# A fused two-block kernel: the attention of block 1 rearranged (one merged tail unit, mask on TensorE, unnormalised differences, LayerNorm and half of the output product inside its steps)

## What is computed

```python
hn = rmsnorm(h, norm1_g[l])
q, k, v, u = split(hn @ w_in[l])                    # 4 heads; q, k: 2 components of 64; v: 128
q, k = apply_rope(q, cos, sin), apply_rope(k, cos, sin)
# differential attention, causal, by head:
s = einsum(q, k) * 0.125 ; s = where(k_pos <= q_pos, s, -inf)
p = softmax(s) ; a = p[:, :, 0] - lam * p[:, :, 1]
attn_out = rmsnorm(a @ v, sub_g) * (1 - lam_init)
# conformer branch: GLU, causal depthwise convolution of width 31, LayerNorm over 512 channels, swish
z = a_half * sigmoid(gate) ; z = conv31(z) + conv_b ; conv_out = silu(layer_norm(z, ln_g, ln_b))
h = h + concat([attn_out, conv_out]) @ w_out[l]     # 1024 x 1024
h = h + (silu(gate) * up) @ w_down[l]               # after a second rmsnorm
```

## Time and profile before

| | us |
|---|---|
| median of 3 runs | 3113.19 (3109.66 to 3121.58) |
| the profiled execution's own time | 3118.58 |
| its span | 3116.8 |
| busy in the span: PE / DVE / ACT / POOL | 2756.3 / 1144.6 / 980.7 / 1205.2 |
| mean granted clock of TensorE | 0.904 of full |

### The profile page before, as it was taken

The page is one execution under the profiler, slowest core; times in us unless marked ns, Lnnn a source line. Parts: engine busy times, 40 slices in busy tenths (PEclk is TensorE's granted clock), DMA queues, the critical chain, the costliest instruction groups (busy, mean ns, idle before and its releaser), DMA issues.

```text
span 3116.8 us, 47600 instructions
## 1 busy us (share of the span) xinstructions
PE 2756.3 (88%) x19056; PEld 2457.3 (79%) x19056; DVE 1144.6 (37%) x1879; ACT 980.7 (31%) x1841; POOL 1205.2 (39%) x511
## 2 busy tenths in 40 slices
PE   5977879999797787999978989889999989699999
PEld 4954879999796477999977868768877777577777
DVE  3874422112268443211224864320266632220110
ACT  2323222222332322222233542123456653221121
POOL 3550335545556023555552431022311135554452
PEclk8975889999898578999987989998999989899999
DMA  3210012232222001223230300031201123222221
GB/s 121 77 54 1 28 54 91 71 108 64 86 70 67 1 14 55 93 72 101 69 96 28 108 28 2 2 95 55 82 27 56 42 91 126 81 68 95 81 94 67
DMA packets 178614, 204.10 MB, mean 65 GB/s; under 512 B 6443, under 2 KB 167174, under 8 KB 178198
## 3 DMA queue, kind: packets, MB, share of 16 engines
q1 hardware_dynamic: 174288, 200.05, 19.9%
q10 hardware_dynamic: 4166, 1.84, 0.2%
HBM read 193.48 MB, written 8.39 MB: 65 GB/s over the span
## 4 chain that ended last, share of the span: by engine, by line
PE 68%; issue 10%; POOL 7%; DVE 7%; ACT 3%; POOLq 2%; DVEq 1%; DMA 1%; ACTq 1%; SPq 0%
PE ps L683 15%; PE ps L684 15%; PE ps L685 15%; PE ps L1431 6%; POOL wlo L2509 5%; PE ps L1321 2%; PE ps L832 2%; DVE top L2086 1%; PE ps L849 1%; PE ps L1303 1%; POOLq L2547 1%; DVE diff L2106 1%; PE ps L1266 1%; POOL hn_lo L2524 1%; PE ps L713 1%
## 5 line engine op out<-in xcount | busy, mean ns | idle before, releaser
L2509 POOL TENSOR_TENSOR wlo<-wraw,whi 128x2048 fp32r<-128x2048 f32 x182 | 836.9, 4599 | 1205.1 <-ACT whi L1498 1185.8
L683 PE MATMUL ps<-hn_hi,whi 128*128 128x264 f32 (+1 forms) x3008 | 972.8, 323 | 64.8 <-POOL hn_lo L2524 31.8
L684 PE MATMUL ps<-hn_lo,whi 128*128 128x264 f32 (+1 forms) x3008 | 958.8, 319 | 0.0
L685 PE MATMUL ps<-hn_hi,wlo 128*128 128x264 f32 (+1 forms) x3008 | 957.1, 318 | 0.0
L683 PEld LDWEIGHTS ps<-hn_hi,whi 128*128 128x128 f32 x3008 | 578.5, 192 | 105.5 <-issue 51.1
L685 PEld LDWEIGHTS ps<-hn_hi,wlo 128*128 128x128 f32 x3008 | 576.9, 192 | 36.4
L684 PEld LDWEIGHTS ps<-hn_lo,whi 128*128 128x128 f32 x3008 | 578.7, 192 | 32.0
L1498 ACT CAST whi<-wraw 128x2048 fp32r<-128x2048 f32 x182 | 346.7, 1905 | 730.5 <-PE ps L685 581.5
L683 PE MATMUL ps<-ff_hi,whi 128*128 128x264 f32 x704 | 200.7, 285 | 9.6 <-POOL ff_lo L2589 9.6
L685 PE MATMUL ps<-ff_hi,wlo 128*128 128x264 f32 x704 | 200.5, 285 | 0.0
L684 PE MATMUL ps<-ff_lo,whi 128*128 128x264 f32 x704 | 200.1, 284 | 0.0
(11 more groups left out here) (406 smaller groups left out, 4157.5 us busy)
## 6 DMA issues: line engine op xcount, KB each, us to landing
wraw<-in_w_in SPq DMA_DIRECT2D x54, 1024.0 KB, 5.3
wraw<-in_w_gate_up SPq DMA_DIRECT2D x44, 1024.0 KB, 5.1
wraw<-in_w_up SPq DMA_DIRECT2D x16, 1024.0 KB, 5.6
wraw<-in_w_down SPq DMA_DIRECT2D x16, 1024.0 KB, 4.9
wraw<-in_w_out SPq DMA_DIRECT2D x12, 1024.0 KB, 5.2
wraw<-in_w_down SPq DMA_DIRECT2D x16, 768.0 KB, 4.6
wraw<-in_w_down SPq DMA_DIRECT2D x16, 640.0 KB, 4.2
gate_dram<-gate_out SPq DMA_DIRECT2D x16, 256.0 KB, 2.1
```

What stands on the lines that cost most here:

```text
L683: nc.tensor.matmul(dst, whi[:, slot, c:c + P], rhs_hi, start=start, stop=False)
L684: nc.tensor.matmul(dst, whi[:, slot, c:c + P], rhs_lo, start=False, stop=False)
L685: return nc.tensor.matmul(dst, wlo[:, slot, c:c + P], rhs_hi, start=False, stop=stop)
L2509: nc.gpsimd.tensor_tensor(wlo[:, slot, :], wraw[:, slot, :], whi[:, slot, :].bitcast(F32), ALU.subtract).then_inc(w_split, 1)
```

## The change

- The four 16-query tiles of the heads become one unit: 17 units in place of 20. The unit stands twelfth (counted from 0) in the list. Its four heads lie in four groups of 32 partitions; the queries are kept in `q_tail`, written by DVE beside the rotary addition.
- The mask is added by PE, as a matmul with the identity behind the scores; DVE takes the maximum with its sign turned, and the scale 0.125 goes into ACT's copy of q, so two of DVE's operations per unit go.
- The first exponential is written in place in PSUM; the difference is (first exponential) + (second) x ratio, not normalised, one DVE operation after a reciprocal and a ratio. The head norm takes up the missing factor through the squared row sums (`mass_sq`).
- Rotations 0 to 2 stand between the last q and k products, rotation 3 behind them, rotations 4 to 7 inside units 1 to 4. The order of the q and k panels follows that.
- 12 taps of channel chunk 1 run on DVE ahead of pass 1's `z`.
- The LayerNorm's spread rows, squares and scaling run inside units 0 and 6 to 8. The output product is cut into 32 halves of 12 matmuls: the conv half of the inner dimension (16 of them) starts at unit 10, one piece in a unit, seven pieces in units 10 to 16; nine stand between the steps of the head norm, and the 16 of the attention half follow. DVE makes 32 additions to `h` instead of 16. The panels of the output weights are cut the other way (4 chunks of rows by 512 columns).
- The transposed differences and the outputs have one PSUM bank each, not two.
- ACT casts the last panel of the output product after the squares, not before.

```diff
@@ PE: what follows the q and k products, and the loop over units
+                            if f >= 23:
+                                rotated(f - 23)
...
+                def rotated(m):
+                    pe.wait_ge(qkv_copied, l * 26 + rot_from[m])
+                    if m:
+                        pe.wait_ge(rope_done, l * KD + m)
+                    if m == 4:
+                        pe.wait_ge(ln_mean_copied, l + 1)
+                    for half in range(2):
+                        last = nc.tensor.matmul(ps[:, rot_bank(m) + half, 0:HALF], rot,
+                                                raw(rot_chunks[m], HALF * half, HALF), start=True, stop=True)
...
+                    if u == TAIL:
+                        for c in range(2):
+                            for h1 in range(HEADS1):
+                                own = slice(32 * h1, 32 * h1 + 32)
+                                q = q_tail[:, c, h1, :]
+                                nc.tensor.matmul(ps[own, c, :], q, raw(4 + h1, 0, 512), start=True, stop=True)
...
                     for c in range(2):
                         own = slice(64 * c, 64 * c + 64)
+                        nc.tensor.matmul(ps[:, 2 * (u % 2) + c, 0:keys], raw(hd, P * t, P)[own, :], raw(4 + hd, 0, keys)[own, :],
+                                         start=True, stop=False, skip_group_check=True)
+                    for c in range(2):
+                        last = nc.tensor.matmul(ps[:, 2 * (u % 2) + c, P * t:keys], ident, causal, start=False, stop=True,
+                                                skip_group_check=True)
...
+                rotated(3)
+                conv_sums()
                 scores(0)
                 scores(1)
+                extras = {0: conv_mean_rows, 6: conv_square_sums, 7: conv_rstd_rows}
+                f = 0
+                for u in range(UNITS1):
+                    differences_turned(u)
+                    if u + 2 < UNITS1:
                         scores(u + 2)
+                    if u in extras:
+                        extras[u]()
+                    elif 1 <= u <= 4:
+                        rotated(u + 3)
+                    elif u >= 10:
+                        out_fill(f)
+                        f += 1
+                    values(u)
...
+                out_fill(7)
+                pe.wait_ge(sub_mass, l + 1)
+                nc.tensor.matmul(ps[:, 4, 0:4 * NT1], ident, mass_sq, start=True, stop=False, skip_group_check=True)
+                head_sums1(0)
+                head_sums1(1)
+                out_fill(8)
+                head_sums1(2)
+                out_fill(9)
+                head_sums1(3)
+                out_fill(10)
+                out_fill(11)
+                head_rows1(0)
+                head_rows1(1)
+                out_fill(12)
+                out_fill(13)
+                head_rows1(2)
+                out_fill(14)
+                head_rows1(3)
+                out_fill(15)
@@ ACT: exponentials
+                            p = probs4[:, u % 2, 1, 0:P * (t + 1)] if c else s[:, 0, :]
+                            last = nc.scalar.activation(p, s[:, c, :], ACT.Exp, bias=top, accum_out=mass[:, c, at:at + 1])
+                    act.drain().then_inc(exp_done, 1)
...
+                for u in range(UNITS1):
+                    if u + 1 < UNITS1:
+                        exponentials(u + 1)
+                    if u:
+                        out_copied(u - 1)
+                    differences_copied(u)
@@ DVE
+                        add_taps(1, range(MERGED))
...
+                    nc.vector.tensor_tensor(turned_half, turned_half, sin.rearrange("p (b n) -> p b n", b=2), ALU.mult)
...
+                    nc.vector.reciprocal(weight[:, slot:slot + 1], mass[:, 1, at:at + 1])
                     dve.drain()
+                    nc.vector.scalar_tensor_tensor(ratio[:, slot:slot + 1], mass[:, 0, at:at + 1], lay_neg_lam,
+                                                   weight[:, slot:slot + 1], ALU.mult, ALU.mult)
                     dve.drain()
+                    nc.vector.scalar_tensor_tensor(diff[:, slot, 0:keys], probs4[:, slot, 1, 0:keys], ratio[:, slot:slot + 1],
+                                                   scores_of(u)[:, 0, :], ALU.mult, ALU.add).then_inc(diff_ready, 1)
...
+                for m in range(4):
+                    rope(m)
                 maxima(0)
+                for u in range(UNITS1):
+                    if u + 1 < UNITS1:
+                        maxima(u + 1)
                     difference(u)
+                    if 1 <= u <= 4:
+                        rope(u + 3)
+                    if u == 6:
                         dve.wait_ge(ln_rms, l + 1)
                         nc.vector.reciprocal(rstd[:, 20:20 + NT1], rms[:, 20:20 + NT1]).then_inc(ln_rstd, 1)
+                    if u == 7:
+                        dve.wait_ge(ln_rows, l + 1)
...
+                    if u >= 11:
+                        out_add(f)
+                        f += 1
@@ POOL (the wait in line 2540 stands as before)
+                    if j == 9:
+                        for m in range(2, 6):
+                            rope_products(m)
                     lower(first + (j + 2), j % 2)
```

More of the change, by code:

```diff
@@ L31 @@
 GROUPS1 = (TAPS - EARLY) // GROUP
[L32 to L33 removed]
+UNITS1 = 4 * HEADS1 + 1
+TAIL = 12
+MERGED = 12
 FF1 = 2816
@@ L816, in _, with conv_sums @@
-                pe.wait_ge(rope_done, l * KD + KD)
-                pe.wait_ge(ln_mean, l + 1)
-                spread(rms, 20, mean_rows).then_inc(ln_mean_rows, 1)
+                def conv_sums():
+                    pe.wait_ge(conv_done, l * 3 + 3)
+                    pe.wait_ge(taps_added, l * GROUPS1 + GROUPS1)
+                    for t in range(NT1):
+                        for c in range(4):
+                            last = nc.tensor.matmul(ps[:, 6, t:t + 1], conv[:, c * T1 + P * t:c * T1 + P * t + P],
+                                                    ones[:, 0:1], start=(t == 0 and c == 0), stop=(c == 3),
+                                                    skip_group_check=True)
+                    last.then_inc(ln_sum, 1)
@@ L2124, in _ @@
+                for f in range(6, 12):
+                    out_add(f)
                 dve.wait_ge(sub_rms, l + 1)
@@ L2561, in _ @@
                 pool.drain()
+                for m in range(6, KD):
+                    rope_products(m)
                 total, part = sq[:, 0, 0:T1], sq[:, 1, 0:T1]
```

531 lines of the change are left out of this document (300 added, 231 removed).

## The result

The changed kernel took 3040.52 us in the median of 4 runs (3038.23 to 3043.26), the kernel before 3113.81 (3109.66 to 3121.58): ratio 0.9765, 95% interval 0.9749 to 0.9781. It is faster by 2.3%; the forecast was 3042. The profiled execution has a span of 3041.4, against 3116.8 before.

A forecast was written before the change was run, and what follows sets the result against it. The prediction took TensorE as the main bound (68% of the chain), in lockstep with VectorE in attention. Terms summed to 35.6 us a layer, 71 for two, giving 3042 us; own range 3022 to 3062, 8-in-10 range 3004 to 3084.

The forecast's parts named there:

- v stall: Before the first v product: GpSimd's third panel waits for a z delayed by 12 taps; loss 9.0 us a layer.
- Rotations: From the last q/k output to the first scores: 26.6 us becomes 9.3, a gain of 17.3 us a layer.
- Units 0 to 4: First units of the attention loop, units 1 to 4 carrying rotations: 40 us, from 42.8 (lower clock) and 33 (upper).
- Units 5 to 9: Plain steps of the attention loop plus LayerNorm: 34 us, from 36.9 at the lower clock and 30 at the upper.
- Units 10 to 16: Loop units with an output-product piece each, including the tail unit: 39 us; 57 at half clock.
- what would make it wrong: Tail unit: the forecast is wrong if its scores take 7 us or more at the upper clock, in turn.
- Clock by the pieces: Attention loop: pieces mixed with short matmuls raise TensorE's clock, PEclk well above 0.55 from unit 10 on.
- Rival 2: Units 0 to 16 and head norm: TensorE becomes the bound at the lower clock, slower at 3130 us; chance 0.08.
- Rival 1: Attention loop: masks, pieces and rotations bring the upper clock from unit 0 on, 3004 us; chance 0.13.
- Behind the loop: From the attention loop's end to the last addition to h: 80.5 us becomes 53.3, a gain of 27.2 a layer.
- Cast order: ScalarE's last output-product cast, 1.90 us, no longer stands ahead of the squares: gain 1.9 us a layer.
- Rival 3: Attention loop: with single PSUM banks, ScalarE's exponentials, copies and outputs in sequence set the step, 3066 us; chance 0.22.

The follow-up runs named there:

- merged_0: The changed kernel with no taps ahead of the second GLU half's z (MERGED = 0, not 12): 3047.39 us, ratio 0.9779 to the kernel before.
- pieces_behind: The changed kernel with the seven output-product pieces behind the attention loop, not inside units 10 to 16: 3075.75 us, ratio 0.9862 to the kernel before.
- before_cast: The kernel before with only ScalarE's last output-product weight cast moved behind its last two squares: 3107.77 us, ratio 0.9968 to the kernel before.

## Why the prediction was right, and where it wasn't

The time was right by 1.5 us, and that is more exact than its terms. The layers gained 14 more than their sum, and start and block 2 gave 9.7 back; the profiled execution was then 2.7 above its median, where I had subtracted 5.4. That all this meets within 1.5 us is luck. Right by mechanism are the parts below that say so. Of these the two largest gains, the rotations and the stretch behind the loop, are read from landmarks alone: no run takes either of them back.

- **v stall: right.** 8.7 for 9.0, by the mechanism given: GpSimd's panel behind the late z (the first v product is 6.2 later, and 2.5 more go by the lower clock behind it). merged_0 shows what the step left out: without the taps the wait moves to the second rotation.
- **Rotations: right**, 17.1 for 17.3, with the sums at 6.07 where I had 5.25.
- **Units 0 to 4: mis-sized.** 35.8 for 40: steps of 5.2, 7.8, 8.3, 8.4 and 6.1, for 6.0, 10.0, 7.8, 8.6 and 8.4. Of the 42.8 at the lower clock and 33 at the upper I took a value near the lower, after the earlier trace rows; the clock was 0.76. Units 1 and 4, where the error lies, ran near the upper level:

```profile
210.36:218.18 7.82, 3.47 (x19) 2.23 (x19) 4.45 (x8) 3.65 (x12) 6.37 (x5) 0.89 0.00 0
234.90:240.99 6.09, 2.93 (x16) 1.95 (x16) 3.06 (x6) 1.21 (x4) 0.00 (x0) 0.95 0.01 3
```

- **Units 5 to 9: right**, 33.1 for 34, at a clock of 0.60. I had counted one table load; four stand there (248.64, 252.23, 255.77, 262.28), for two in the loop before.
- **Units 10 to 16: the sum near, the step wrong.** 41.5 for 39. I read the 32 records in 0.4 us of the earlier trace rows as groups side by side, whatever stands between them. Here they ran in turn, 8.8 us for 3.4 measured side by side; the 3.4 is what I had given for two rounds at half clock, and that is how they then ran (0.56). The prediction named this as what would make it wrong (7 us or more at the upper clock), and it happened. That step took 12.5 and not 6; the sum held because I had taken 36 for steps that add up to 33.3, and 3 more for the tail.
- **Clock by the pieces: right.** It is 0.88 from 275 to 315 and 1.00 from 315 to 343. pieces_behind shows the cause and prices it at 5 (medians) to 13 us (its profile) a layer; the prediction had 21 between its two levels in the loop alone, and I take it that Rival 2 would have needed more than the level of that experiment. Rival 1, the upper clock from unit 0 on, didn't come: 0.76 in units 0 to 4, 0.60 in units 5 to 9.
- **Behind the loop: near**, 28.7 for 27.2.
- **Cast order: half.** 1.9 for the cast (2.0 in before_cast), and 1.3 for a table load that goes as SiLU moves ahead of the head norm. The prediction doesn't have the load that the norm loses.
- **Rival 3** (ScalarE's ring): not seen. TensorE's only wait for a turned copy in the loop of layer 0 is 0.83, in unit 8.
- **Not in the forecast:** block 2, untouched, differs by 22 us between profiles.

## What to carry to other kernels

Before pricing an edit at the wait that it removes, look for the due time of the work that it displaces: taps taken from ahead of v came back one for one as a wait for the rotation, and placing them in the engine's idle gaps gained 1 to 4 us of that stretch, with nothing to see in the total. In this chain, which alternates between TensorE and VectorE, dense independent matmuls put between were worth more than their own time, since the granted clock around them rose; and 6.3 us of added VectorE work cost a layer 14 to 16. Group matmuls for different output partitions next to each other, with nothing short between. And read a gain of a few microseconds by landmarks in the profile, when untouched stages of the same program vary by more.

## What the runs showed of the hardware that I had not expected

- Eight matmuls with 32 output partitions each and 512 columns took 3.4 us in four groups side by side, at a granted clock of 0.56, and 8.8 when each group's own short matmuls followed it, at 0.84.
- A stretch of block 2 with the same 12014 matmul records took 1910.8 to 1933.2 us in the profiles of these kernels, with TensorE busy 1742 to 1765 and 228 to 278 us at a granted clock of 0.50: stretches at the lower clock came and went with no edit near.
- VectorE's `ratio` (128x1, 0.22 us) took 0.87 at 216.56, with GpSimd at a rotary product (1.29 at 216.13), while the maximum over PSUM ahead of it kept its 1.22. All three long cases of the loop (0.87, 0.91 and 0.87, at 216.56, 224.73 and 233.56) end within 0.02 us of the end of the operation that GpSimd had running (217.42, 225.63, 234.41): it looks as if `ratio` waited for it and did not run slower. That is argued from these three cases; no run tests it.
